# mLSTM scan of a two-layer token mixer: state terms and decayed scores one step ahead, the output-gate projection behind the scan without a barrier, another order of weight loads

## The chip, the cores and the metric

The kernel runs on one core of one Trainium2 chip. The core has five engines, each with its own instruction queue: TensorE (PE), VectorE (DVE), ScalarE (ACT), GpSimd (POOL) and SyncE (SP), which issues most of the DMA transfers. The metric is the device time of one execution in microseconds (us). The kernel before takes 2833.85 us, the median of three executions (2833.59 to 2839.1).

## The reference

A trunk of two layers works on 512 latent tokens and 256 context tokens of width 1024, in float32. Each layer has a token mixer and a mixture of 16 experts. The mixer projects its normalised input with one wide matrix (`w_in`) into the inputs of three branches: a bidirectional chunkwise mLSTM, a pooling mixer, and a neighbourhood attention. The change lies in the mLSTM and in the loads around it. One step of its scan is, for one direction and one chunk of 128 tokens:

```
b = cumsum(f); dmat = where(tril, b_t - b_s + i_s, -inf)
g = b + m;     mt = maximum(g, dmat.max(-1))
sc  = (q @ k.T) * exp(dmat - mt)                    # scores times decay: "S x D"
num = exp(g - mt) * (C @ q) + sc @ v                # C @ q: the state term, "qC"
den = exp(g - mt) * (n @ q) + sc.sum(-1)
h   = num / maximum(abs(den), exp(-mt))
C   = decay * C + sum_s ws_s * v_s k_s^T            # n likewise
out = sigmoid(o) * head_rms(h_forward + h_backward) # o: the output-gate projection
```

There are four heads, two directions and six chunks (two of context, then four latent; the backward direction goes through both sets in reverse). Layer 0 needs the output of every chunk; layer 1 needs only those of the four latent chunks, its context chunks serving for the state alone. The expert part gathers 64 latent rows per expert (in layer 0 also 32 context rows), runs a SwiGLU with three 1024 x 1024 matrices and adds the weighted rows to a buffer in DRAM.

## The kernel before, in words

The code is five queues written out by hand, one per engine, tied by semaphores. A layer is cut into phases. At the end of each, every engine drains its queue, adds one to the semaphore `phase` and waits until all four compute engines have (`phase_end`, L330 to L332). In a profile such a wait stands as L331 of the engine that came last.

A projection with a 1024 x 512 piece of `w_in` is done in two halves of 512 rows. A half is loaded by SP into a slot (1 MB), split into a rounded high part by ACT (`split`, L896) and a low part by POOL (L1612), and multiplied three times over (high x high, high x low, low x high, L409 and L414). There are three ring slots for weights. They hold, one after another, the halves of `w_in` (called qk, v, o, kn, qn, vn, pu after the branch they feed; o is the output gate, kn, qn and vn the attention's keys, queries and values, pu the pooling input) and twelve 2 MB pieces of the modulation weights (`ada`, L423). A load is issued by SP when the last user of its slot has signalled (`released`), and SP's queue is in order: a load whose slot is not free holds everything behind it.

The scan (phase 4) runs over n = 0 to 11: step n//2 of direction n%2. For an n with an output, the engines do this:

- PE: with eight of the n, one ada piece of 64 matmuls in pairs of partitions (L423); the state term qC into banks 2 and 3 (L577); the state's update kv from POOL's weighted values into bank 6 (L587); then the scores times values (`m_num`, L594) into banks 2 and 3 again, after ACT has taken qC out of them and DVE has written S x D; then the scores of the next output (L559).
- ACT: the scaled copy `qcs` of qC (four instructions, L997), the four exponentials of the next output's decay matrix (L984), and the broadcast load of a row of numbers for a later one (`u_load`, L946).
- DVE: S x D (L1344), the update of the state C (L1352, two), the sum nd of qcs and num (L1357), the denominator (L1360 to L1362), and the quotient into `hsum` (one instruction for the first direction to reach a chunk, L1365, four for the second, L1368).
- POOL: the masked rows for the decay (`masked`, L1633), the weighted values (L1643), and at the scan's end the low parts of the two halves of w_o.

After `phase_end(4)` the o projection runs over token tiles (6 in layer 0, 4 in layer 1), its first half of rows for all tiles and then its second. In the second half each tile is followed by `head_cols` of the tile before (L606), four transposes that need `hfin` from DVE (L1384), which needs the norm of `hsum` (L1373 to L1380) and ACT's sigmoid (L1017). Phases 5 and 6 end it and the projections kn, qn and vn. In the vn projection's second half ACT copies each finished tile out (L1058, L1060), the first four through POOL's DMA to `v_dram` (L1660) by way of two staging buffers; ACT's split of the second half of pu stands in its queue behind the wait for the second tile, and POOL's low part of it behind the fourth DMA.

In the expert loop six slots take the six 2 MB units of an expert. SP waits until the unit that used the slot is done, and then also until the load before the last one has landed, before it issues the next:

```
s2, back = (s - 2) % 6, 1 if s < 2 else 0
sp.wait_ge(w_ready(s2), 16 * e + 16 * (moe_base[l][s2] + 1 - back))
```

Of the kernel before, what the change touches and what calls it, by code (L numbers as in the profile page):

```python
# [4 lines left out]
F32 = mybir.dt.float32  # L5
# [69 lines left out]
def build(nc, A, out):  # L75
    ctx = ExitStack()
    with ctx:
# [121 lines left out]
        qcs = cut(zone, 28976, "p (h n) -> p h n", 516, h=MH)  # L199
# [82 lines left out]

        moe_base = []
        for l in range(DEPTH):
            n = [0]

            def nxt(key, src):
                add((l,) + key, src, n[0] % 3, None)
                n[0] += 1
            for j in range(4):  # L290
                nxt(("ada", l, j), kn512(ada[l], 512 * j))
            for name, c in (("qk", C_QK), ("v", C_V), ("o", C_O), ("kn", C_KN), ("qn", C_QN), ("vn", C_VN),
                            ("pu", C_PU)):
                for half in range(2):
                    nxt((name, half), w_in[l][512 * half:512 * half + 512, c:c + 512].rearrange("(k p) n -> p k n", p=P))
                if name == "v":
                    for j in range(4, 12):
                        nxt(("ada", l, j), kn512(ada[l], 512 * j))
            assert n[0] % 3 == 2
# [33 lines left out]
        NPH = 12  # L333
# [55 lines left out]
        def _(pe):  # L389
# [48 lines left out]
            for l in range(DEPTH):  # L438
# [114 lines left out]
                def pair_scores(u):  # L553
# [7 lines left out]
                    i.then_inc(sem("m_s"), 1)  # L561
                pair_scores(0)
                for n in range(12):
                    st, r = n // 2, n % 2
                    c = (FW, BWD)[r][st]
                    for j in range(4 + 2 * n // 3, 4 + 2 * (n + 1) // 3):
                        ada_unit(l, j, 1 if j < 8 else 0)
                    outp = c < nt(l)
                    if outp:
                        u = outs.index((r, c))  # L570
                        if st:
                            pe.wait_ge(sem("m_C"), l * PER["m_C"] + n - 1)
                        if u:
                            pe.wait_ge(sem("m_nd"), l * PER["m_nd"] + u)
                        for h in range(MH):
                            q0 = 64 * (h % 2)
                            i = mm(bank(2 + h % 2)[:, (h // 2) * 129:(h // 2) * 129 + 129],  # L577
                                   qT[q0:q0 + 64, h // 2, c * P:(c + 1) * P], Cst[q0:q0 + 64, r, h // 2, :],
                                   start=True, stop=True)
                        i.then_inc(sem("m_qc"), 1)  # L580
# [1318 lines left out]
```

## Time and profile before

| what | value |
|---|---|
| median of three executions | 2833.85 us |
| the profiled execution, its own time | 2833.22 us |
| its span, first to last instruction | 2831.1 us |
| mean granted TensorE clock, share of full speed | 0.937 |
| layer 0: scan's first kv to the o projection's first matmul | 152.77 to 230.72 us |
| layer 1: the same | 1682.42 to 1744.35 us |

All times of the trace are microseconds from the start of the span. 2.1 us of the profiled execution lie outside its span. In the rows further down, the chain of waits is the work that ended last, followed backwards and printed in order of time: start, duration, engine and line, with a count of merged instructions. "PEclk" is the TensorE clock that was granted: 1.00 is 2.4 GHz, 0.50 is 1.2 GHz.

### The profile page before, as it was taken

What the parts mean: (1) busy time and instruction counts of PE and PEld (TensorE: products, weight loads), DVE (VectorE), ACT (ScalarE), POOL (GpSimd) and SP (SyncE); (2) the same over time, 40 slices, a digit from 0 to 9 for tenths busy, and PEclk for the clock granted to TensorE, in tenths of its full rate; (3) what the DMA queues carried; (4) which work ended last, traced back from release to release, by engine and by line L of the source; (5) the groups of instructions that cost most, each with busy time, mean ns of one, the idle gap of its engine ahead of it and who ended that gap; (6) DMA issues with size and microseconds to landing.
All of it is one profiled execution on the core that took longest, in us unless ns stands there. A gap on an engine that the chain in (4) does not pass through costs nothing.

```text
span 2831.1 us, 38214 instructions
## 1 busy us (share of the span) xinstructions
PE 2411.7 (85%) x15894; PEld 1558.4 (55%) x15894; DVE 659.9 (23%) x1326; ACT 610.7 (22%) x1018; POOL 577.7 (20%) x320
## 2 busy tenths in 40 slices
PE   3987989899999499999997597988899868877775
PEld 2766867788884244444443476776688432322222
DVE  3255045311001511111111426046210130000002
ACT  3233233212111211111111424232321211000101
POOL 1133231224420001111111223331454000001000
PEclk7999999999999699999999799999999979999997
DMA  6261330111230589999999244431222469999997
GB/s 221 86 228 59 119 97 27 53 53 60 67 129 27 204 310 381 386 391 389 388 389 366 89 166 173 133 97 54 70 90 97 131 263 401 407 405 404 405 407 296
DMA packets 180453, 603.11 MB, mean 213 GB/s; under 512 B 14328, under 2 KB 55680, under 8 KB 167872
## 3 DMA queue, kind: packets, MB, share of 16 engines
q1 hardware_dynamic: 164704, 566.16, 53.2%
q0 software_dynamic: 12608, 30.19, 4.2%
q10 hardware_dynamic: 3040, 5.31, 0.6%
q8 instruction: 77, 1.26, 0.2%
q14 instruction: 24, 0.20, 0.0%
HBM read 579.51 MB, written 28.39 MB: 215 GB/s over the span
## 4 chain that ended last, share of the span: by engine, by line
PE 42%; DMA 37%; issue 8%; DVE 7%; ACT 3%; POOL 1%; SPq 1%; POOLq 1%; ACTq 0%; DVEq 0%
PE ps L414 15%; DMA ring_lo<-in_w_gate 12%; DMA zone<-in_w_down 10%; PE ps L409 9%; DMA zone<-in_w_up 6%; DMA ring_lo<-in_w_up 6%; PE ps L749 6%; PE ps L767 5%; PE ps L423 1%; PE ps L825 1%; DMA ring_lo<-in_ada_w 1%; DVE small L1417 1%; POOLq L331 1%; POOL zone L1676 1%; PE ps L594 1%
## 5 line engine op out<-in xcount | busy, mean ns | idle before, releaser
L825 PE MATMUL ps<-ring_lo,zone 128*32 128x256 f32 (+1 forms) x3072 | 460.1, 509 | 75.7 <-DMA ring_lo<-in_w_gate 43.2
L414 PE MATMUL ps<-hi_r,ring_r 128*128 128x512 f32 (+1 forms) x1792 | 477.3, 355 | 17.4 <-POOLq L331 14.8
L825 PEld LDWEIGHTS ps<-ring_lo,zone 128*32 128x32 f32 (+1 forms) x3072 | 167.1, 127 | 365.3 <-issue 337.8
L414 PEld LDWEIGHTS ps<-hi_r,ring_r 128*128 128x128 f32 x1792 | 318.8, 191 | 66.6 <-POOLq L331 16.5
L1612 POOL TENSOR_TENSOR ring_r<-ring_lo,ring_r 128x2048 fp32r<-128x2048 f32 x52 | 239.5, 4610 | 478.1 <-ACT ring_r L896 477.8
L414 PE MATMUL ps<-lo_r,ring_r 128*128 128x512 f32 (+1 forms) x896 | 316.7, 353 | 0.0
L835 PE MATMUL ps<-zone 128*64 128x512 f32 (+1 forms) x2048 | 289.6, 493 | 0.9
L409 PE MATMUL ps<-ring_r,hi_r 128*128 128x512 f32 x736 | 234.1, 400 | 21.7 <-DVEq L331 21.7
L835 PEld LDWEIGHTS ps<-zone 128*64 128x64 f32 (+1 forms) x2048 | 111.3, 124 | 162.3 <-issue 141.5
L1716 POOL DMA_INDIRECT zone<-xn_dram,zone x36 | 40.9, 1137 | 753.0 <-DVE zone L1587 667.3
L414 PEld LDWEIGHTS ps<-lo_r,ring_r 128*128 128x128 f32 x896 | 170.7, 191 | 23.7
L409 PEld LDWEIGHTS ps<-ring_r,hi_r 128*128 128x128 f32 x736 | 138.0, 191 | 50.9 <-DVEq L331 22.1
L825 PE MATMUL ps<-zone 128*32 128x256 f32 (+1 forms) x1024 | 146.8, 487 | 16.2 <-DMA zone<-in_w_up 16.2
L409 PE MATMUL ps<-ring_r,lo_r 128*128 128x512 f32 x368 | 145.2, 395 | 0.0
L1570 DVE COPY zone<-zone 128x2 f32 (+1 forms) x32 | 5.1, 161 | 593.0 <-POOLq L1737 593.0
L1486 DVE TENSOR_TENSOR zone<-zone,ps 128x768 f32<-128x768 f32 (+1 forms) x48 | 39.4, 821 | 426.4 <-ACT zone L1118 426.4
L767 PE MATMUL ps<-ring_lo,zone 128*128 128x512 f32 x320 | 137.7, 592 | 0.0
L1733 POOL DMA_INDIRECT moe_dram<-zone x48 | 74.9, 1559 | 273.1 <-issue 273.1
L749 PE MATMUL ps<-br_lo,ring_r 128*128 128x512 f32 (+1 forms) x480 | 125.7, 354 | 0.0
L896 ACT ACTIVATE ring_r<-ring_lo 128x2048 fp32r<-128x2048 f32 x48 | 91.7, 1915 | 133.5 <-DMA ring_lo<-in_w_in 112.8
L825 PEld LDWEIGHTS ps<-zone 128*32 128x32 f32 (+1 forms) x1024 | 56.6, 123 | 100.6 <-issue 89.4
L749 PE MATMUL ps<-br_up,ring_r 128*128 128x512 f32 (+1 forms) x384 | 103.1, 355 | 3.2 <-DVE br_lo L1478 3.2
(260 smaller groups left out, 2549.0 us busy)
## 6 DMA issues: line engine op xcount, KB each, us to landing
ring_lo<-in_w_gate SPq DMA_DIRECT2D x64, 2048.0 KB
zone<-in_w_down SPq DMA_DIRECT2D x64, 2048.0 KB, 10.1
ring_lo<-in_w_up SPq DMA_DIRECT2D x32, 2048.0 KB
zone<-in_w_up SPq DMA_DIRECT2D x32, 2048.0 KB, 11.7
ring_lo<-in_w_in SPq DMA_DIRECT2D x52, 1024.0 KB
ring_lo<-in_ada_w SPq DMA_DIRECT2D x24, 2048.0 KB
ring_lo<-in_w_branch SPq DMA_DIRECT2D x24, 512.0 KB, 6.1
zone<-v_dram SPq DMA_DIRECT2D x128, 64.0 KB, 1.9
```

Source lines behind the costliest of these rows:

```text
L331: eng.drain().then_inc(sem("phase"), 1)
L409: i = mm(dst, a[:, k, t * P:(t + 1) * P], b[:, kk, :], start=start and n == 0, stop=stop and n == 2)
L414: i = mm(dst[:, t0:t0 + tw], b[:, kk, f * P:(f + 1) * P], a[:, k, t0:t0 + tw], start=start and n == 0, stop=stop and n == 2)
L749: i = mm(pb[:, t0:t0 + tw], w[:, k, (f % 2) * P:(f % 2 + 1) * P], b[:, k, t0:t0 + tw], start=(k == 0 and x == 0), stop=(k == KB - 1 and x ...
L767: i = mm(PS[2 + t % 2][:, j * 512:(j + 1) * 512], acc[:, k, t * P:(t + 1) * P], w[:, k, :], start=(k == 0), stop=(k == KD - 1))
L825: i = mm(bank(((2, 4), (3, 5))[s // 2][gi])[j * M:(j + 1) * M, 0:W], xeT[:, k, c0:c0 + M], w[:, k % 4, j * W:(j + 1) * W], start=(k == 0), ...
L835: i = mm(bank((3, 5)[gi])[j * M:(j + 1) * M, 0:W], hidL[:, k % 4, k // 4, :] if gi == 0 else hidC[:, k % 2, k // 2, :], w[:, k % 4, j * W: ...
L896: A_(unit_hi(slot, ring_r), unit_lo(slot), ACT.Copy).then_inc(sem("w_hi"), 1)
L1486: V.tensor_tensor(dst[:, 0:TW(l)], sg[f % 2][:, 0:TW(l)], PS[(f % 2) * 2][:, 0:TW(l)], ALU.mult).then_inc(sem("mg_free"), 1)
L1612: G.tensor_tensor(unit_lo(slot, ring_r), unit_lo(slot), unit_hi(slot, ring_r).bitcast(F32), ALU.subtract)\
L1716: G.indirect_dma_start(xe[0:ns, :], None, xn_dram[l][0:TW(l), :], bass.IndirectOffsetOnAxis(ap=icur[0:ns, 0:1], axis=0)).then_inc(sem("xe_ ...
L1733: G.indirect_dma_start(moe_dram[l][0:TW(l), :].rearrange("t (j n) -> (t j) n", n=W), bass.IndirectOffsetOnAxis(ap=iprev[:, g:g + 1], axis= ...
```

## The change

The scan is reordered. PE issues the state term of n + 1 right behind the num of n, and the scores of the next output before this num; num gets banks 0 and 1 of its own. `qcs` has two buffers. DVE writes S x D of the next output ahead of the sum nd of this one. ACT has two decay matrices done before the barrier ahead of the scan, POOL three masked rows. The ada pieces stand at the end of eight steps, all in bank 7. The barrier between scan and o projection is gone (11 phases for 12); the o projection waits for single semaphores and uses banks 6, 7, 0, 1, 2, 3. POOL's low parts of w_o are made in four pieces of 512 columns each, the first one's inside the scan; ACT's `split(6)`, which works on kn's first half, now follows `split(5)` with no barrier between.

The loads have a table `ORDER` in place of a running count modulo three. o's first half is now loaded ahead of three of the ada pieces. By this table some halves get other slots: kn's first half takes the slot of o's first half, which is released when PE has finished the first half of the o projection (before: that of the last ada piece), and pu's second half takes slot 0, the one of vn's second half (before: the slot of vn's first half).

SP's second wait in the expert loop, on the load before the last one, is removed.

```diff
-        qcs = cut(zone, 28976, "p (h n) -> p h n", 516, h=MH)
+        qcs = [cut(zone, at_, "p (h n) -> p h n", 516, h=MH) for at_ in (28976, 27952)]
...
+        ORDER = ((("ada", 0), 0), (("ada", 1), 1), (("ada", 2), 2), (("ada", 3), 0), (("qk", 0), 1), (("qk", 1), 2), (("v", 0), 0),
...
+                 (("qn", 1), 1), (("vn", 0), 2), (("vn", 1), 0), (("pu", 0), 1), (("pu", 1), 0))
+        ADA_STEP = {0: 4, 1: 5, 2: 6, 4: 7, 5: 8, 7: 9, 8: 10, 10: 11}
+        O_BANKS = (6, 7, 0, 1, 2, 3)
...
+                def state_terms(n):
+                    st, r = n // 2, n % 2
+                    c = (FW, BWD)[r][st]
+                    u = outs.index((r, c))
+                    if st:
+                        pe.wait_ge(sem("m_C"), l * PER["m_C"] + n - 1)
+                    if u:
+                        pe.wait_ge(sem("m_qcs"), l * PER["m_qcs"] + u)
...
+                    if n in steps_out:
+                        u = outs.index((r, c))
                         if u + 1 < len(outs):
                             pair_scores(u + 1)
-                phase_end(pe, ph + 4)
+                        else:
+                            pe.wait_ge(sem("m_sd"), l * PER["m_sd"] + u + 1)
+                        if u:
+                            pe.wait_ge(sem("m_nd"), l * PER["m_nd"] + u)
+                        for h in range(MH):
+                            i = mm(bank(h % 2)[:, (h // 2) * 129:(h // 2) * 129 + 129], sdT[u % 2][:, h * P:(h + 1) * P],
+                                   v_ext[:, c, h, :], start=True, stop=True)
+                        i.then_inc(sem("m_num"), 1)
+                    if n + 1 in steps_out:
+                        state_terms(n + 1)
+                    if n in ADA_STEP:
+                        if ADA_STEP[n] == 8:
+                            pe.wait_ge(sem("ada_rows"), 3 * l + 2)
+                        ada_unit(l, ADA_STEP[n], 7)
...
+                    if n == 8:
+                        split(l, 4)
+                ada_rows(l, 2, 7)
                 split(l, 5)
-                phase_end(act, ph + 4)
                 split(l, 6)
...
+                def decayed_scores(u):
+                    dve.wait_ge(sem("m_s"), l * PER["m_s"] + u + 1)
+                    dve.wait_ge(sem("m_D"), l * PER["m_D"] + u + 1)
+                    V.tensor_tensor(by_parity(sdT[u % 2]), two(PS[2], P), by_parity(U[u % 3]), ALU.mult)\
+                        .then_inc(sem("m_sd"), 1)
...
+                w = 2048 // parts
+                for x in range(parts):
+                    i = G.tensor_tensor(unit_lo(slot, ring_r)[:, x * w:x * w + w], unit_lo(slot)[:, x * w:x * w + w],
+                                        unit_hi(slot, ring_r)[:, x * w:x * w + w].bitcast(F32), ALU.subtract)
+                i.then_inc(sem("w_lo"), 1)
...
+                    if n == 8:
+                        split(l, 4, 4)
+                split(l, 5, 4)
                 split(l, 6)
                 split(l, 7)
-                phase_end(pool, ph + 5)
+                phase_end(pool, ph + 4)
...
-
-                        s2, back = (s - 2) % 6, 1 if s < 2 else 0
-                        sp.wait_ge(w_ready(s2), 16 * e + 16 * (moe_base[l][s2] + 1 - back))
-                        sp.sem_inc(sem("sp_turn"), 1)
                         expert_unit(e, s)
```

PE's queue inside the scan of layer 0, before: one step with an ada piece (L423), its state term (L577), kv (L587), num (L594) and the next scores (L559).

```order
L423 MATMUL ps<-ring_lo,small 32x128 [waits w_ready2]
L423 MATMUL ps<-ring_lo,small 32x128 x31
L577 MATMUL ps<-zone 128x129 [waits m_nd,m_C]
L577 MATMUL ps<-zone 128x129 x3
L587 MATMUL ps<-zone 64x129 [waits m_C,m_vw]
L587 MATMUL ps<-zone 64x129 x3
L594 MATMUL ps<-zone 128x129 [waits m_qcs,m_sd]
L594 MATMUL ps<-zone 128x129 x3
L559 MATMUL ps<-zone 128x128 [waits m_sd]
L559 MATMUL ps<-zone 128x128 x3
```

The same place now: kv (L592), the next scores (L561), num (L604), the next state term (L575), and before them the ada piece of the step ahead (L425).

```order
L425 MATMUL ps<-ring_lo,small 32x128 [waits w_ready0,ada_rows]
L425 MATMUL ps<-ring_lo,small 32x128 x31
L592 MATMUL ps<-zone 64x129 [waits m_C,m_vw]
L592 MATMUL ps<-zone 64x129 x3
L561 MATMUL ps<-zone 128x128 [waits m_sd]
L561 MATMUL ps<-zone 128x128 x3
L604 MATMUL ps<-zone 128x129 [waits m_nd]
L604 MATMUL ps<-zone 128x129 x3
L575 MATMUL ps<-zone 128x129 [waits m_qcs,m_C]
L575 MATMUL ps<-zone 128x129 x3
```

The scores moved ahead of num and the state term behind it. num waits for the sum nd of the output before, no more for `qcs`.

SP's queue in layer 0, before, from the five ada loads of the scan to the first attention value load. The halves from `w_in` are o, o, kn (three waiting for ada_done), kn (half), qn (oproj), qn (half), vn (np), then behind the tables vn (half), pu (np) and pu (half), and the first piece of the merge weights (128x8x256).

```order
L1752 DMA ring_lo<-in_ada_w 128x8x512 [waits ada_done] x5
L1752 DMA ring_lo<-in_w_in 128x4x512 [waits ada_done] x3
L1752 DMA ring_lo<-in_w_in 128x4x512 [waits half]
L1752 DMA ring_lo<-in_w_in 128x4x512 [waits oproj]
L1752 DMA ring_lo<-in_w_in 128x4x512 [waits half]
L1752 DMA ring_lo<-in_w_in 128x4x512 [waits np]
...
L1752 DMA ring_lo<-in_w_in 128x4x512 [waits half]
L1752 DMA ring_lo<-in_w_in 128x4x512 [waits np]
L1752 DMA ring_lo<-in_w_in 128x4x512 [waits half]
L1752 DMA ring_lo<-in_w_in 128x8x256 [waits np]
L1778 DMA zone<-v_dram 32x512 [waits v_out1,v_out0]
```

SP's queue now, the same stretch.

```order
L1785 DMA ring_lo<-in_ada_w 128x8x512 [waits ada_done] x2
L1785 DMA ring_lo<-in_w_in 128x4x512 [waits ada_done]
L1785 DMA ring_lo<-in_ada_w 128x8x512 [waits ada_done] x3
L1785 DMA ring_lo<-in_w_in 128x4x512 [waits ada_done]
L1785 DMA ring_lo<-in_w_in 128x4x512 [waits half]
L1785 DMA ring_lo<-in_w_in 128x4x512 [waits ada_done]
L1785 DMA ring_lo<-in_w_in 128x4x512 [waits oproj]
...
L1785 DMA ring_lo<-in_w_in 128x4x512 [waits half]
L1785 DMA ring_lo<-in_w_in 128x4x512 [waits np] x2
L1785 DMA ring_lo<-in_w_in 128x8x256 [waits half]
```

kn's first half, the load behind o's second, waits for `half` (the end of the first half of the o projection) where it waited for an ada piece, and pu's second half waits for `np` (the last vn tile) where it waited for `half` (the end of vn's first half).

ACT's queue now, in the vn projection of layer 0: the copies out of the tiles, with the split of pu's second half (L917) between the first and the second. It stood at the same place before.

```order
L1080 ACTIVATE zone<-ps 128x512 [waits np]
L917 ACTIVATE ring_r<-ring_lo 128x2048 [waits w_ready0,np]
L1080 ACTIVATE zone<-ps 128x512
L1080 ACTIVATE zone<-ps 128x512 [waits v_out0,np]
L1080 ACTIVATE zone<-ps 128x512 [waits v_out1,np]
L1082 ACTIVATE zone<-ps 128x512 [waits np] x2
```

What moved is only the slot: the split waits for `w_ready0`, so for a load into the slot of vn's second half.

## Rows read from the trace of the kernel before

**Rows 1.** Chain of waits, layer 0: start, duration (us), engine, line, count.
```profile
152.77 1.13 PE ps L587 x8
196.65 1.13 PE ps L594 x8
197.78 0.65 PE ps L559 x8
198.43 1.88 PE ps L423 x64
200.31 0.67 PE ps L577 x8
218.72 1.14 PE ps L594 x8
221.30 9.33 DVE zone L1368 x4
230.72 24.84 PE ps L409 x96
272.78 67.15 PE ps L414 x384
339.93 16.36 PE ps L409 x72
```

**Rows 2.** Chain of waits, layer 1.
```profile
1682.42 1.13 PE ps L587 x8
1732.35 1.14 PE ps L594 x8
1744.35 18.70 PE ps L409 x72
1775.74 57.22 PE ps L414 x288
```

**Rows 3.** Stretches: bounds, length, busy us of each engine, PEclk, DMA share, GB/s.
```profile
175.00:205.00 30.00, 25.83 (x433) 21.41 (x432) 19.99 (x45) 11.98 (x41) 11.60 (x10) 0.94 0.80 283
230.00:236.00 6.00, 5.28 (x12) 4.18 (x13) 5.72 (x8) 3.19 (x2) 3.25 (x1) 0.50 0.00 0
```

**Rows 4.** Instructions of DVE: start, duration, line, operands, count.
```profile
204.19 0.86 DVE L1360 SCALAR_TENSOR_TENSOR small<-zone 128x4 f32<-128x4 f32 x1
262.74 3.70 DVE L1384 TENSOR_TENSOR zone<-zone 128x512 f32<-128x512 f32 x1 [1.90 <-ACT zone L1017]
```

**Rows 5.** Issues of SP, three merged: the first at 339.96.
```profile
339.96 33.93 SPq L1752 DMA_DIRECT2D ring_lo<-in_w_in  x3
```

**Rows 6.** Instructions of ACT, with idle time before them and its releaser.
```profile
232.63 1.28 ACT L1019 ACT_TABLE_LOAD   x1
243.01 0.32 ACT L1019 ACTIVATE small<-small 128x24 f32<-128x24 f32 x1 [9.10 <-DVEq L1375]
345.09 1.92 ACT L896 ACTIVATE ring_r<-ring_lo 128x2048 fp32r<-128x2048 f32 x1 [4.25 <-DMA ring_lo<-in_w_in]
373.54 0.60 ACT L1060 ACTIVATE zone<-ps 128x512 f32<-128x512 f32 x1 [2.12 <-PE ps L409]
```

**Rows 7.** Instructions of POOL in layer 0.
```profile
365.36 0.58 POOL L1660 DMA_DIRECT2D v_dram<-zone  x1 [3.74 <-ACT zone L1058]
369.55 4.61 POOL L1612 TENSOR_TENSOR ring_r<-ring_lo,ring_r 128x2048 fp32r<-128x2048 f32 x1
```

**Rows 8.** DMA issues of the page: KB each, median us from issue to landing.
```profile
v_dram<-zone POOLq DMA_DIRECT2D x8, 256.0 KB, 2.3
```

**Rows 9.** Stretches of the expert part, columns as in rows 3.
```profile
952.00:962.00 10.00, 6.62 (x38) 6.12 (x36) 8.22 (x18) 2.05 (x2) 0.00 (x0) 0.75 1.03 421
1317.00:1386.00 69.00, 67.33 (x608) 28.90 (x606) 7.85 (x22) 7.83 (x12) 8.10 (x6) 1.00 1.03 388
1338.00:1352.00 14.00, 13.13 (x116) 6.01 (x114) 2.87 (x9) 0.60 (x1) 0.22 (x1) 1.00 1.03 414
2559.00:2571.00 12.00, 9.55 (x37) 3.79 (x37) 0.97 (x3) 1.44 (x2) 0.00 (x0) 0.86 1.00 426
```

More of the change, by code:

```diff
@@ L561, in pair_scores @@
                     i.then_inc(sem("m_s"), 1)
+                def state_terms(n):
[7 more added lines that the diff above has]
+                    for h in range(MH):
+                        q0 = 64 * (h % 2)
+                        i = mm(bank(2 + h % 2)[:, (h // 2) * 129:(h // 2) * 129 + 129],
+                               qT[q0:q0 + 64, h // 2, c * P:(c + 1) * P], Cst[q0:q0 + 64, r, h // 2, :],
+                               start=True, stop=True)
+                    i.then_inc(sem("m_qc"), 1)
+                steps_out = [n for n in range(12) if (FW, BWD)[n % 2][n // 2] < nt(l)]
                 pair_scores(0)
+                if 0 in steps_out:
+                    state_terms(0)
                 for n in range(12):
@@ L987, in _ @@
                 decays(0)
+                decays(1)
+                phase_end(act, ph + 3)
                 for n in range(12):
@@ L991, in _ @@
                         u = outs.index((r, c))
-                        act.wait_ge(sem("m_qc"), l * PER["m_qc"] + u + 1)
-                        if u:
-                            act.wait_ge(sem("m_nd"), l * PER["m_nd"] + u)
-                        for h in range(MH):
-                            x0 = 129 * (h // 2)
-                            i = A_(qcs[:, h, :], bank(2 + h % 2)[:, x0:x0 + 129], ACT.Copy,
-                                   scale=xp0[:, r, 4 * (n // 2) + h:4 * (n // 2) + h + 1])
-                        i.then_inc(sem("m_qcs"), 1)
-                        if u + 1 < len(outs):
-                            decays(u + 1)
                         if u + 3 < len(outs):
@@ L1004, in _ @@
                             u_load(u + 3)
-                    if n == 6:
-                        ada_rows(l, 1, 1)
-                ada_rows(l, 2, 0)
-                split(l, 4)
+                        act.wait_ge(sem("m_qc"), l * PER["m_qc"] + u + 1)
+                        if u >= 2:
+                            act.wait_ge(sem("m_nd"), l * PER["m_nd"] + u - 1)
+                        for h in range(MH):
+                            x0 = 129 * (h // 2)
+                            i = A_(qcs[u % 2][:, h, :], bank(2 + h % 2)[:, x0:x0 + 129], ACT.Copy,
+                                   scale=xp0[:, r, 4 * (n // 2) + h:4 * (n // 2) + h + 1])
+                        i.then_inc(sem("m_qcs"), 1)
+                        if u + 2 < len(outs):
+                            decays(u + 2)
+                    if n == 5:
+                        ada_rows(l, 1, 7)
+                    if n == 8:
+                        split(l, 4)
+                ada_rows(l, 2, 7)
                 split(l, 5)
-                phase_end(act, ph + 4)
                 split(l, 6)
@@ L1602, in _, with split @@
             G = nc.gpsimd
-            def split(l, h):
+            def split(l, h, parts=1):
                 slot = units[(l,) + SPLITS[h]][1]
```

181 lines of the change are left out of this document (81 added, 100 removed).

## The prediction

> **What bounds the kernel now.** I read the chain of waits first, in order of time, and looked for stretches of the mixer in which PE doesn't follow PE. The scan of layer 0 is a relay: a step with an ada piece runs num, scores, ada piece, state term (1.13, 0.65, 1.88, 0.67 us) on PE, then waits for ACT's copy before the next num [rows 1]. From the first kv (152.77) to the end of the last num (219.86) it takes 67.1 us for twelve steps, 5.6 each; in layer 1, where four steps have no output, 51.1 us (1682.42 to 1733.49) [rows 1, 2]. The table of stretches shows that no engine is full there: of 30 us PE works 25.8 and DVE 20.0 [rows 3]. Behind each scan stands a hole of 10.9 us (219.86 to 230.72, 1733.49 to 1744.35): four small DVE instructions of the last step take 9.33 us beside POOL's low parts of w_o, and everybody waits at the barrier [rows 1, 2]. The o projection then starts at the lower of TensorE's two clock levels, 1.2 GHz (granted 0.50 in the first 6 us) [rows 3]. Its first 96 matmuls take 24.84 us; at 16.36/72 = 0.227 us each they would take 21.8 [rows 1].
>
> Next I followed the queues behind this place, ACT's and SP's, because the change alters which slot a half comes into. In the vn projection nothing waits for a load now: PE finishes its last tile at 373.54, POOL its low part of pu at 374.16, and the barrier falls 0.6 us behind PE [rows 6, 7].
>
> Last the expert part, most of the second and fourth quarter of the span. There the DMA engines are full (share 1.03) and in layer 0 PE too, 67.3 of 69 us [rows 9].
>
> **The change part by part.** All in the time of the profiled execution: 2831.1 us of span and 2.1 outside.
>
> *Scan.* A step with an ada piece becomes a PE queue without a wait: kv, scores, num, state term, ada piece. kv has no row of its own at full clock; as four matmuls of 129 columns like the state term I take 0.67. Sum 0.67 + 0.65 + 1.13 + 0.67 + 1.88 = 5.00 us. A step without one would take PE 3.1, but DVE worked 20.0 us in 30/5.6 = 5.4 steps, 3.7 us per step, and will be the longer one; with some waiting, 4.0. Layer 0: eight ada steps less one kv, 39.3; three of 4.0; last num 1.1: 52.5. The first step runs at the lower clock (its kv takes 1.13 now [rows 1]): about double, + 3.8. POOL's four pieces lie in steps 9 and 10; + 2. So 58.3, a gain of 8.8. Layer 1: three steps of kv and ada piece (7.7), one of kv and state term (1.3), four of 5.0, two of 4.0, 4.3 and 1.1, 42.4; cold 2.2, pieces 2: 46.6, a gain of 4.5. Together 13. The start itself I take as even: two masked rows go ahead of the barrier on POOL and as many exponentials on ACT. Bounds: nothing gained, if rows that are loaded for the decay now come late, to 27, if the steps are PE's alone and warm. 13 is between, nearest to the durations of rows 1.
>
> *Barrier.* With no phase end the o projection follows the last num. Its low part is made around step 9, and its first banks are free. Gain 2 x 10.9 = 21.7. PE stays warm: 24.84 - 21.8 = 3.0, and 18.70 - 72 x 0.227 = 2.3 in layer 1 [rows 1, 2]. Together 27. DVE's tail (its four quotients and the squares of hsum) now lies beside the first half of the o projection, 6 x 12 x 0.227 = 16.4 us in layer 0 and 10.9 in layer 1.
>
> *What is late next: kn's first half.* Its load waits for the end H of the o projection's first half, and ACT's split of it stands in ACT's queue ahead of the square root and of every sigmoid that the o projection's second half needs. A load of this kind issued at 339.96 was used at 345.09: 5.1 us [rows 5, 6]. Split 1.9, so H + 7.1. Then POOL makes the low part, 4.6, in one piece, and DVE's two instructions for `hfin` (scale and product, both with two inputs in SBUF) wait for it: H + 11.7, and 0.6 + 0.7 more (an instruction on 512 columns takes 0.6 on ACT [rows 6]; I take about that for DVE): H + 13.0. PE stands at `head_cols(0)` after two tiles, H + 5.5. It waits 7.5 us, and then I let it run at the lower clock as after the hole of before, 3 us. The later stall of before (3.70 us for a product beside POOL [rows 4]) I leave as it was. Cost 2 x 10.5 = 21. Bounds: 5 us per layer if DVE isn't held and PE stays warm, 13 if more waits.
>
> The rows behind this: a DVE instruction on four columns that takes 0.86 us [rows 4], and the 9.33 us of four on 128 columns [rows 1], each with two inputs in SBUF and each beside a POOL instruction. The Trainium skill ("SBUF — State Buffer", section "SBUF: two separate sides") says that VectorE with two SBUF inputs and GpSimd share a port pair as an exclusive lock for a whole instruction. The trace agrees. It speaks for the four pieces and against the uncut low part of kn that now starts just before `hfin`. By it hfin(0) comes at H + 13.0; without it, after table loads of 1.28 and a root of 0.32 [rows 6], at about H + 11, and the stall is 5.5 in place of 7.5, 4 us less over both layers.
>
> *pu's second half.* Its slot is now that of vn's second half, so SP can't load it before PE's last vn tile, T. But ACT's split of it stands behind the first of six copies. From T: load 5.1, split 1.9, copy of tile 1 0.5, to POOL's issue 0.3, transfer to `v_dram` 2.3 [rows 8] (the fourth copy needs this staging buffer), copy 0.7, 0.3, POOL's issue 0.6, and POOL's low part of pu, 4.6, which stands behind the DMAs [rows 7]. T + 16.3 in place of T + 0.6: 15.7 us per layer, 31 together. Nothing hides it: the barrier waits for ACT and POOL, and the attention starts behind it. Bounds: 28 (DMA latencies half hidden) to 35. The first load of the merge weights also waits longer, for the end of pu's projection, but the pooling on DVE is ahead of its use; cost nothing, or 3 us without that cover.
>
> *Expert loads.* SP's extra wait goes, so up to five loads are under way in place of two. With five and fewer under way at 952 to 962 the engines moved 421 GB/s at a share of 1.03; with two and no indirect transfer 414 in layer 0 and 426 in layer 1, shares 1.03 and 1.00 [rows 9]. The engines are full either way, and the bytes are the same: nothing. Bounds: layer 0 can gain what PE is idle, 1.7 of 69 us, 12 us over 15 experts; on the other side, the indirect transfers hold the mean down to 388 from 414, 6%, and if they were held up by a quarter as much again it would be 15 us.
>
> Sum: - 13 - 27 + 21 + 31 = + 12. The profiled execution would go from 2833.2 to 2845.3, and the median lies 0.6 above it: **2846 us**.
>
> **Rivals.**
> - *Deeper load queue pays.* For it: 421 over 414. Against it: layer 1 already has 426 with two under way, and the share is full. It would give layer 0 back 12 us: 2834. The Trainium skill ("DMA: Bandwidth & Descriptors", section "Where 436 GB/s comes from") has 436 GB/s as the ceiling of the 16 engines. By that layer 0 has 5% over its 414, more than PE's idle share lets it use, so PE's 12 us stay the limit.
> - *pu's load is not waited for.* If ACT's split is served in time, because vn's last tiles don't end what the slot's release waits for, the 31 us go and the change does what its words say: 2815, faster. Against it: the wait `w_ready0` in ACT's queue and `np` in SP's, both in the order of instructions. What decides is whether the load is issued before or after PE's last vn tile.
> - *Expert part slower.* Five loads ahead of gathers and read-add transfers: POOL's rows come late, 0.5 us per expert, 15 over 30: 2861. It decides once an expert's rows land after PE's last down matmul of the one before. Against it: nothing waits for them now.
> - *The scan doesn't speed up.* DVE held by POOL at each step, and the rows for the decays late: the 13 us shrink to 3: 2856.
> - *Both small stalls fall short.* The scan gains 20 and the stall at kn costs 14: 2832 to 2838.
>
> **How the numbers follow.** Forecast 0.54; deeper queue 0.13; no wait for pu's load 0.05; experts slower 0.09; scan no faster 0.11; small stalls short 0.08. About 0.2% (5.7 us) is what a measurement of this kernel can tell from no change. Faster than 2828.2: the second rival, 0.05, and a part of the first, of the last and of a sum of them, 0.10: 0.15. Within: the rest of the first and the last, and the lower edge of the forecast, 0.17. Slower 0.68. The range for 8 in 10 is 2829 to 2861; the forecast's own, from the bounds of stalls and scan, is 2838 to 2858.
>
> **What would show it.** In the profile after: no DVE instruction of 9 us and no hole before the o projection; num to num 5 us in the scan; PE idle about 7.5 us before `head_cols(0)` in both layers, released by DVE; ACT idle in front of its split of pu until 5 us after PE's last vn tile, and PE idle 16 us behind this tile; two experts of layer 0 in 69 us. I am wrong if PE follows on within 2 us after vn, or if the period of the experts moves by over 0.3 us.

## The result and the profile after

| | before | after |
|---|---|---|
| median of 13 executions each | 2834.84 us | 2840.72 us |
| ratio after to before, 95% interval | | 1.0019 [1.0011, 1.0028] |
| profiled execution, its span | 2831.1 us | 2835.4 us |
| mean granted clock | 0.937 | 0.935 |
| layer 0: scan's first kv to the o projection's first matmul | 78.0 us | 52.0 us |
| layer 1: the same | 61.9 us | 45.7 us |

The changed kernel is 0.19% slower, 5.4 us by the ratio, where 0.43% was forecast (2846); the time lies inside the range, and at the 0.2% that a measurement can tell. The stretch that the change is about became 42 us shorter, so some 46 us came in elsewhere.

The chain of waits of the changed kernel in layer 0, from the first kv to kn's first matmul (L592 is kv, L604 num, L411 the o projection, L619 the head transposes; it answers to [rows 1]):

```profile
153.32 1.06 PE ps L592 x8
...
163.09 6.63 DMA zone<-u_dram
...
171.81 6.28 DMA zone<-u_dram
...
181.34 1.95 PE ps L425 x64
...
204.21 1.13 PE ps L604 x8
205.34 16.36 PE ps L411 x72
...
221.72 5.14 DMA ring_lo<-in_w_in
...
226.88 1.91 ACT ring_r L917
...
228.81 1.28 ACT L1041
...
230.79 3.14 DVE zone L1406
...
233.95 0.70 DVE zone L1410
...
234.70 1.12 PE ps L619 x4
235.81 4.41 PE ps L411 x12
```

The hole of [rows 1] is gone: num ends at 205.34 and the o projection starts in the same moment, its 72 matmuls at 0.227 us each. Its first half ends at 221.70 (H), PE has two more tiles (to 227.2) and then waits; the first head transposes start at 234.70: H + 13.0, the number of the forecast. In layer 1 H is 1734.72 and they start at 1747.78, H + 13.1. Between lies the load of kn's first half, ACT's split of it, the square root and DVE's scale (L1406), which takes 3.14 us beside POOL's low part. The stretches of that wait and behind it (columns as in [rows 3]) have PE empty for 7.5 us, the size forecast, and then 6 us at a mean clock of 0.62:

```profile
227.20:234.70 7.50, 0.00 (x1) 0.01 (x1) 4.18 (x4) 5.56 (x6) 4.50 (x1) 0.85 0.21 80
234.70:240.70 6.00, 6.00 (x21) 5.02 (x22) 1.83 (x3) 1.04 (x2) 0.00 (x0) 0.62 0.00 0
```

Kn itself starts at 254.23, against 272.78 in [rows 1]. The scan of layer 1, whose last num ends at 1723.77 (it answers to [rows 2]), has a wait for an ada load in it:

```profile
1700.50 13.15 DMA ring_lo<-in_ada_w
...
1723.77 10.95 PE ps L411 x48
```

The same chain at the end of vn in layer 0 (it answers to [rows 6, 7]):

```profile
338.61 16.38 PE ps L411 x72
...
355.01 5.30 DMA ring_lo<-in_w_in
...
363.09 2.35 DMA v_dram<-zone
...
366.42 0.54 POOL v_dram L1693
366.96 4.94 POOLq L333
```

PE is done at 354.99 (T). Then everything is as the queue of ACT has it: load, split, copies, transfer, and POOL's low part, until 371.90, T + 16.9. In layer 1 it is T + 17.0. In the kernel before, PE paused here for 1.1 us in either layer (373.50 to 374.62 in layer 0; the 0.6 us of the prediction goes by the end of POOL's instruction, and the barrier opens 0.5 us behind that).

In the expert part of layer 0, the stretch of [rows 9] (columns as there):

```profile
1317.00:1386.00 69.00, 68.90 (x616) 29.46 (x614) 7.68 (x20) 7.83 (x12) 8.10 (x6) 1.00 1.03 391
```

PE is idle 0.1 us of 69 instead of 1.7, and the loads move 391 GB/s instead of 388.

From the start of one stage to the start of the next, the difference of the two profiled executions comes out like this (us, after less before; the o projection runs from its first matmul to kn's first, and "behind vn" is PE's pause between its last vn matmul and its next one):

| | layer 0 | layer 1 |
|---|---|---|
| scan | 52.0 - 67.1 = - 15.1 | 45.7 - 51.1 = - 5.4 |
| hole behind it | - 10.9 | - 10.9 |
| o projection | 48.9 - 42.1 = + 6.8 | 38.1 - 31.4 = + 6.7 |
| behind vn | 16.9 - 1.1 = + 15.8 | 17.0 - 1.1 = + 15.9 |
| experts, first to last matmul of gate and up | 528.0 - 532.1 = - 4.1 | 489.3 - 488.5 = + 0.8 |
| all other stretches | about + 5 over both | |

The named stages sum to - 0.4, and the spans differ by + 4.3, so all of the difference stands in the last row. That row is many small differences of 0.3 to 1.7 us between stages whose code is the same (the largest are the attention of layer 0, + 1.7, and of layer 1, + 1.0, and the way from layer 0's experts to layer 1's scan, + 1.0); it has no single cause that I could find.

### The profile page after: what moved, and what is told of

Its sections match the earlier page's. It is cut to its first block, busy times and chain, and to the rows that moved or that the text cites. A ratio compares the mean times of both kernels' runs of the same rounds, so it can differ in the third digit from the quotient of the medians.

```text
span 2835.4 us, 37864 instructions
## 1 busy us (share of the span) xinstructions
PE 2407.3 (85%) x15894; PEld 1555.2 (55%) x15894; DVE 654.6 (23%) x1326; ACT 611.2 (22%) x1018; POOL 581.1 (20%) x332
## 4 chain that ended last, share of the span: by engine, by line
PE 59%; DMA 21%; issue 8%; DVE 6%; ACT 3%; POOL 1%; SPq 1%; POOLq 1%; ACTq 0%; DVEq 0%
PE ps L416 15%; PE ps L846 14%; DMA ring_lo<-in_w_up 13%; PE ps L411 9%; PE ps L770 6%; PE ps L856 5%; PE ps L788 5%; DMA zone<-in_w_up 4%; DMA ring_lo<-in_ada_w 2%; PE ps L425 1%; POOLq L333 1%; DVE small L1443 1%; POOL zone L1709 1%; DMA ring_lo<-in_w_in 1%; PE ps L710 1%
## 5 line engine op out<-in xcount | busy, mean ns | idle before, releaser
L1640 POOL TENSOR_TENSOR ring_r<-ring_lo,ring_r 128x2048 fp32r<-128x2048 f32 (+1 forms) x64 | 241.6, 3784 | 467.2 <-ACT ring_r L917 466.9
L411 PE MATMUL ps<-ring_r,hi_r 128*128 128x512 f32 x736 | 232.6, 397 | 0.0
L1749 POOL DMA_INDIRECT zone<-xn_dram,zone x36 | 40.9, 1136 | 754.2 <-DVE zone L1613 667.6
L411 PEld LDWEIGHTS ps<-ring_r,hi_r 128*128 128x128 f32 x736 | 137.3, 190 | 28.5 <-issue 0.8
L411 PE MATMUL ps<-ring_r,lo_r 128*128 128x512 f32 x368 | 144.6, 393 | 0.0
L917 ACT ACTIVATE ring_r<-ring_lo 128x2048 fp32r<-128x2048 f32 x48 | 91.8, 1912 | 190.0 <-DMA ring_lo<-in_w_in 189.6
## 6 DMA issues: line engine op xcount, KB each, us to landing
ring_lo<-in_w_up SPq DMA_DIRECT2D x32, 2048.0 KB, 21.6
zone<-in_w_up SPq DMA_DIRECT2D x32, 2048.0 KB, 26.4
```

The source lines that it names most:

```text
L411: i = mm(dst, a[:, k, t * P:(t + 1) * P], b[:, kk, :], start=start and n == 0, stop=stop and n == 2)
L917: A_(unit_hi(slot, ring_r), unit_lo(slot), ACT.Copy).then_inc(sem("w_hi"), 1)
L1640: i = G.tensor_tensor(unit_lo(slot, ring_r)[:, x * w:x * w + w], unit_lo(slot)[:, x * w:x * w + w], unit_hi(slot, ring_r)[:, x * w:x * w + ...
L1749: G.indirect_dma_start(xe[0:ns, :], None, xn_dram[l][0:TW(l), :], bass.IndirectOffsetOnAxis(ap=icur[0:ns, 0:1], axis=0)).then_inc(sem("xe_ ...
```

## The experiments

A ratio is always to the kernel before on the same chip, and 1.0019 is the changed kernel's. 0.001 is 2.8 us.

**Expert loads alone.** The kernel before, with this taken out of SP's loop:

```
-    s2, back = (s - 2) % 6, 1 if s < 2 else 0
-    sp.wait_ge(w_ready(s2), 16 * e + 16 * (moe_base[l][s2] + 1 - back))
-    sp.sem_inc(sem("sp_turn"), 1)
```

> The kernel before with SP's second wait in the expert loop taken out and nothing else, so that five expert loads can be under way instead of two. My theory: the traces of before and after show layer 0's period fall from 34.4 to 33.4 us in most experts and layer 1's stay at 32.3, so about 3 us faster than before, all of it in layer 0's experts, nothing in layer 1 (2830 to 2833). Rival 1 (the forecast's own term): the engines are full either way, no difference to before within 1 us. Rival 2 (the gain in the changed kernel's experts comes from something else, such as an earlier start of the stage): no difference either, and the period of layer 0 stays at 34.4 us. Rival 3 (deeper queue pays in full): 12 us faster, 2823.

Measured: 2831.2, ratio 0.9983 [0.9972, 0.9994], 3 to 5 us faster than before. The chain of layer 0's experts in this kernel shows one expert from L835 to L835, 33.41 us, all of it PE:

```profile
1046.56 10.68 PE ps L835 x96
1057.24 21.22 PE ps L825 x192
1079.97 5.34 PE ps L835 x23
```

The chain of before, in a later part, passes only loads, one after the other, 34.4 us for each expert:

```profile
1317.56 11.90 DMA ring_lo<-in_w_gate
1329.60 11.96 DMA zone<-in_w_up
1341.73 10.08 DMA zone<-in_w_down
1352.02 11.80 DMA ring_lo<-in_w_gate
```

But the kernel before doesn't run at 34.4 us all along. From the start of one expert's gate matmuls to the next one's, it too takes PE's own 33.4 us for its second to ninth expert, and 34.1 to 34.5 for the six periods behind them; from 1000 to 1270 us PE is busy 269.6 of 270. Without the wait the 33.4 us last for eleven experts, here and in the changed kernel. Behind them the changed kernel's chain goes back to a load (26.6 us from issue to landing) and a period of 34.2. So in both kernels experts are served from a store of finished loads until it is used up, and then the engines' rate counts. The longer queue makes the store last three experts longer.

The throttle thus cost layer 0 about 4 us and layer 1 nothing that can be told (the changed kernel is 0.8 us longer there), and the rival that the queue pays the full 12 is wrong too. My forecast's zero was read from a share of 1.03, which hid those 1.7 us of idle PE that its own bound had named; and the bound of 12 took these 69 us for a sample of all 15 periods, where PE was idle in six.

**pu's split moved behind what needs ACT and POOL.**

```
 (ACT, vn copies)
-    if t == 1:
-        split(l, 13)
 (ACT, attention, step n)
+    if n == 3:
+        split(l, 13)
 (POOL: split(l, 13) from ahead of the barrier behind vn to behind the last bias)
```

> The changed kernel with the split of pu's second half moved to where it is no longer waited for at the end of the vn projection: ACT's part behind the fourth step of the attention, POOL's behind its last bias of the attention. Slots and loads stay as they are. My theory: the 16.9 and 17.0 us between PE's last vn tile and the barrier shrink to about 6 (copies of the last tiles and their transfers to DRAM still stand in front of it: 0.5 + 2.3 + 0.7 + 0.3 us and the POOL issue) or less, ACT pays up to 1.9 us in the attention: 20 to 31 us faster than the changed kernel, 2810 to 2821. Rival (the wait only moves: the attention's first loads or the pool step are late next): under 10 us. The stall in front of the first head transposes, 7.6 us per layer, stays.

Measured: 2820.76, ratio 0.9962 [0.9949, 0.9976], 16 us less than the changed kernel. The wait is gone: PE's last tile is finished at 353.4 and the barrier falls at 354.0. But 32 us went there, and the kernel is only 16 us faster. Of the rest some 13 are seen in the attention, which from this barrier to POOL's next instruction behind it (L1713) took 116.5 us; in the changed kernel it took 110.5, and in layer 1 95.5 against 88.0. The rows of the eighth kernel below, which has POOL's part at the same place, show where.

**Another table of slots.**

```
-    (("ada", 9), 2), (("ada", 10), 0), (("ada", 11), 2), (("o", 1), 0), (("kn", 0), 1), (("kn", 1), 2), (("qn", 0), 0),
-    (("qn", 1), 1), (("vn", 0), 2), (("vn", 1), 0), (("pu", 0), 1), (("pu", 1), 0))
+    (("ada", 9), 2), (("ada", 10), 0), (("o", 1), 2), (("ada", 11), 0), (("kn", 0), 0), (("kn", 1), 1), (("qn", 0), 2),
+    (("qn", 1), 0), (("vn", 0), 1), (("vn", 1), 2), (("pu", 0), 0), (("pu", 1), 1))
```

> The changed kernel with another table of slots: o's second half takes the slot of ada piece 9, so that kn's first half has the slot of the last ada piece and not of o's first half, and pu's second half has the slot of vn's first. Both are then loaded at least half a projection before ACT's split asks for them. My theory: the hole before the first head transposes (7.6 us and 2 us at the lower clock per layer) and the 16 us behind vn both go: 20 + 32 = up to 50 us less than the changed kernel, but DVE's product stays beside POOL's low parts somewhere, and a late low part of qn or vn may cost some: 2790 to 2800. Rival 1 (kn's stall comes from DVE's tail beside POOL, not from the load): only the 32 us of pu go: 2808, and PE still idle 7 us in front of the first head transposes. Rival 2 (only slots move the waits to qn or vn): over 2815.

Measured: 2800.76, ratio 0.9878 [0.9863, 0.9893], 40 us less than the changed kernel and 34 less than before. Both late loads go: in layer 0 the o projection takes 40.2 us instead of 48.9, and the barrier falls 1 us behind PE's last vn tile. The forecast's two minus terms were therefore real, and its two plus terms are the price of slots, not of the scheme. It falls short of the 50 in two places. The o projection yields 13 us of the 20 (layer 1: 34.0 us instead of 38.1): it still has DVE's 3.7 us product, and in layer 0 DVE's four last quotients take 7.3 us beside the pieces of w_o's second half and kn's uncut low part right behind them (5.0 in the tenth kernel, where kn's is in pieces too). And the table makes a new wait: ada piece 11 is loaded into the slot that piece 10 has just left. The chain of its scan in layer 0:

```profile
182.68 11.67 DMA ring_lo<-in_ada_w
194.40 2.00 PE ps L425 x64
196.41 7.62 DMA ring_lo<-in_ada_w
204.07 2.94 PE ps L425 x64
```

The scan takes 55.7 us there instead of 52.0, and 47.4 instead of 45.7 in layer 1.

**kn's first low part in four pieces.** In the changed kernel:

```
-    split(l, 6)
+    split(l, 6, 4)
```

> The changed kernel with POOL's low part of kn's first half made in four pieces instead of one; the load stays as late as it is. DVE's two instructions for the first output tile now wait behind the one long POOL instruction (first tile ready 13.0 us after the end H of the o projection's first half in both layers). My theory, which the Trainium skill's page "SBUF — State Buffer" (section "SBUF: two separate sides") supports with a lock held for one whole instruction: DVE gets in between two pieces, the first tile is ready at H + 10 to 11, the stall in front of the head transposes shrinks from 7.6 to about 5, and the kernel is 4 to 5 us faster than the changed one (2836), if the low part's own longer duration doesn't eat it. Rival (the load sets the stall alone, DVE isn't held): no difference, first tile at H + 13.

Measured: 2837.69, ratio 1.0019 [1.0008, 1.0029], the changed kernel's. Both theories are half right. DVE's rows (start, duration, operands) first of the changed kernel and then of this one:

```profile
230.79 3.13 DVE L1406 TENSOR_TENSOR zone<-zone,small 128x512 f32<-128x512 f32 x1
233.95 0.69 DVE L1410 TENSOR_TENSOR zone<-zone 128x512 f32<-128x512 f32 x1
```

```profile
231.19 1.11 DVE L1406 TENSOR_TENSOR zone<-zone,small 128x512 f32<-128x512 f32 x1
232.84 1.14 DVE L1410 TENSOR_TENSOR zone<-zone 128x512 f32<-128x512 f32 x1 [0.54 <-ACT zone L1039]
...
244.02 3.69 DVE L1410 TENSOR_TENSOR zone<-zone 128x512 f32<-128x512 f32 x1 [1.92 <-ACT zone L1039]
```

Beside pieces the scale takes 1.11 us instead of 3.13, so the trace bears out the rule of the Trainium skill ("SBUF — State Buffer", section "SBUF: two separate sides") that the lock lasts one whole instruction. But then DVE waits 0.54 us for ACT's sigmoid, which stands behind a second table load of 1.28 us, and its product takes 1.14 us beside a piece: the first tile comes at H + 11.8 instead of H + 13.0. And the 3.7 us beside the low part of kn's second half is still there. The long instruction was worth 1 us here, and nothing in the total, because two other things were nearly as late.

**The barrier put back.** The changed kernel with

```
+    phase_end(pe, ph + 4)      (and on DVE, ACT and POOL; later phases + 1)
```

> The changed kernel with the phase end between the scan and the o projection put back on the four compute engines (PE behind the last ada piece, DVE behind the last quotients, ACT and POOL behind their split of o's second half); the order of the scan, the slots and the pieces stay. This measures the forecast's term of 27 us for the barrier by itself. My theory: DVE's tail of the last step ends 6.2 us behind the last num in the profile of the changed kernel (205.34 to 211.5), and PE restarts at the lower clock (2 to 3 us): 8 to 9 us per layer, 16 to 18 slower than the changed kernel, 2857. The forecast's term would want 27, 2868. Rival (the hole is only moved, because kn's late load and DVE's tail are paid behind the barrier anyway): under 8 us, 2848 or less.

Measured: 2858.41, ratio 1.0086 [1.006, 1.0113], 19 us above the changed kernel. Its chains in layer 0 and layer 1:

```profile
208.43 2.90 DVE zone L1397 x4
...
211.42 18.24 PE ps L411 x72
```

```profile
1736.68 5.13 DVE zone L1397 x4
...
1741.91 13.80 PE ps L411 x48
```

The hole is 6.3 and 6.8 us and the o projection's first half is 1.9 and 2.9 us longer, since it starts at the lower clock: 17.8. So the barrier by itself is worth 18. The rest of the forecast's 27 is DVE's shorter tail: the four DVE instructions had already gone from 9.33 us [rows 1] to 2.9 and 5.1. Two things did that, and no run parts them cleanly. Before, the tail stood beside both low parts of w_o (220.94 to 229.94 on POOL); now the first of them is made inside the scan. And the second is in pieces. In the sixth kernel, where the first is as early and the second is in one instruction, the four take 5.46 us in layer 0. By that some 4 us of the 6.4 come from the earlier first half, and 2.5 from the pieces.

**The pieces taken away.** The changed kernel with `split(l, 4, 4)` and `split(l, 5, 4)` turned to `split(l, 4)` and `split(l, 5)` on POOL.

> The changed kernel with the low parts of both halves of w_o made by POOL in one instruction each instead of four. My theory: DVE's two-input instructions of steps 9 and 10 and of the tail wait up to 4 us behind each; the first falls in the scan, where PE waits for DVE, 2 to 4 us per layer; the second in DVE's tail, which nothing waits for now: 4 to 8 us slower than the changed kernel, 2845 to 2849. Rival (the barrier's removal alone took the held instructions off the path, the pieces are worth nothing): the same time within 2 us.

Measured: 2845.71, ratio 1.0035 [1.0019, 1.0051], 4.5 us above the changed kernel, though the two intervals overlap. Its chain in layer 0:

```profile
194.49 6.39 DVE zone L1395 x4
...
202.89 1.81 PE ps L604 x8
```

Four quotients take 6.39 us beside POOL's first low part, PE waits for them before its eleventh num, and the scan 55.0 us instead of 52.0; in layer 1 it takes 49.3 instead of 45.7.

**A full rotation, and what can be added to it.** Ada pieces 9 to 11 come ahead of o's halves, and the split of o's first half one step later:

```
+    (("ada", 9), 1), (("ada", 10), 2), (("ada", 11), 0), (("o", 0), 1), (("o", 1), 2), (("kn", 0), 0), (("kn", 1), 1), (("qn", 0), 2),
+    (("qn", 1), 0), (("vn", 0), 1), (("vn", 1), 2), (("pu", 0), 0), (("pu", 1), 1))
```

> The changed kernel with another table: ada pieces 9 to 11 are loaded ahead of o's halves and all halves rotate through the slots (o's first half follows ada piece 9, its second ada piece 10, kn's first ada piece 11, pu's second vn's first); ACT's and POOL's split of o's first half stand one step later. In the table of the third experiment ada piece 11 had the slot of ada piece 10, and the chain of waits there showed PE waiting for two ada loads of 11.7 and 7.6 us (span 2802.8). My theory: these waits go, 3 to 4 us in layer 0 and 1 to 3 in layer 1, so 4 to 7 us less than with that table, 2794 to 2797, if the load of o's first half, now issued after step 7, is in before the last num. Rival (loads of this part share the DMA engines with the decay rows, and the sum of bytes sets the end of the scan): the same 2801, or slower, if o's first half comes late.

Measured: 2800.71, ratio 0.9876 [0.9852, 0.9899]: the same as the third kernel. In layer 0 the scan takes 51.3 us instead of 55.7. In layer 1 it takes 50.4 instead of 47.4: its chain passes 11.05 us of the load of o's first half, which ACT's split waits for ahead of the next copies `qcs`. That is the last clause of the rival, o's first half coming late.

The eighth kernel has `split(l, 6, 4)` and `split(l, 7, 4)`, and POOL's `split(l, 13)` behind its attention loop:

> As the kernel of the seventh experiment, and POOL makes the low part of pu's second half behind its attention loop instead of ahead of the barrier behind vn, and kn's low parts in four pieces each. My theory: the barrier behind vn falls about 1 us behind PE's last tile and not 6.7 us as in the third experiment (345.8 to 352.4), 5 us per layer; and DVE's product of the second output tile (3.7 us) takes 1 to 1.5 us: 2 us per layer. Together 12 to 14 us less than the seventh experiment: 2781 to 2785. Rival (POOL's later low part or the pieces hold DVE's masks and maxima in the attention or kn's own start): only 5 to 6 us less.

Measured: 2801.32, ratio 0.9882 [0.9861, 0.9904]. My reading of the third kernel's tail was wrong: I had taken an ACT copy at 345.8 for PE's last tile, which ends at 351. There was 1 us to win, not 5. And the low part inside the attention costs. DVE's rows beside it (first fence), and PE's next 16 matmuls of L710, with the same 16 later in the attention (second fence):

```profile
417.66 4.98 DVE L1453 TENSOR_SCALAR zone<-cst,small 128x128 f32<-128x128 f32 x2
422.56 0.68 DVE L1465 COPY zone<-ps 128x512 f32<-128x512 f32 x1
```

```profile
425.36 3.71 PE ps L710 x16
...
436.02 2.00 PE ps L710 x16
```

This pair takes 0.48 us where no POOL instruction stands beside it (426.75), and 0.72 beside one of POOL's short biases. PE stands idle meanwhile, from 418.77 to 423.38, and then runs at a granted clock of 0.50 until 429.07, the level of 1.2 GHz: its 32 matmuls of L727 and L710 take 5.69 us, and 3.08 in the tenth kernel, where nothing held DVE. The attention took 116.4 us, as in the second kernel, against 108.6 in the seventh. Some 4.3 us of that are the pair's, and 2.6 the lower clock's.

The tenth kernel takes that one move back and keeps kn's pieces:

> The kernel of the seventh experiment with kn's low parts in four pieces each, and POOL's low part of pu back at its place ahead of the barrier behind vn. In the eighth experiment the attention of layer 0 took 116.4 us between its barriers instead of 108.4, and vn's barrier fell only 1.6 us behind PE's last tile in the seventh. My theory: POOL's low part inside the attention cost the eighth what the pieces won: DVE's product of the second tile no longer takes 3.7 us, 2 to 3 us per layer, so 4 to 6 us less than the seventh, 2795 to 2797. Rival (the pieces win nothing, as in the fourth experiment, since something else comes last): 2801.

Measured: 2792.70, ratio 0.9852 [0.9832, 0.9872]: the fastest here, 42 us below before and 47 below the changed kernel. Its chain at the head transposes of layer 0 (L411 x12 is one output tile):

```profile
228.52 2.74 PE ps L411 x12
...
231.69 2.76 PE ps L411 x12
...
238.07 2.78 PE ps L411 x12
...
243.73 6.50 PE ps L416 x26
```

No stall of 3.7 us and no lower clock is left. The o projection takes 38.2 us in layer 0 and 29 in layer 1 (40.9 and 34 in the seventh kernel, 48.9 and 38.1 in the changed one). The pieces that were worth nothing with a late load are worth 7 to 8 us without it, by the traces and by the medians; the two timed intervals overlap.

**Decay rows loaded earlier.** Four buffers instead of three, first in the changed kernel, then in the tenth:

```
-    U = [... for i in range(3)]
+    U = [... for i in range(3)] + [cut(zone, 6656, None, 512)]
-    if u + 3 < len(outs): ... u_load(u + 3)
+    if u + 4 < len(outs): ... u_load(u + 4)
```

> The changed kernel with four buffers for the decay rows of the scan instead of three (the fourth in a part of the zone that is free there), so that a row is loaded one output earlier; nothing else changes. In the profile of the changed kernel the chain of waits of layer 0's scan passes two loads of decay rows (6.6 and 6.3 us) with POOL's mask and ACT's exponentials behind each, and PE stands until 181.3; in layer 1 it passes one ada load instead. My theory: these rows, requested too late, are what keeps the scan of layer 0 at 52.0 us instead of some 43 (eight ada steps of 4.9, three of 3.1 and the last num, less a kv): one of the two loads goes, so 4 to 8 us less in layer 0, 0 to 2 in layer 1: 2833 to 2837. Rival 1 (ada loads are behind them and come in at their own pace): less than 2 us. Rival 2 (the four first rows now share the engines with the ada loads and each takes longer): 2 us more.

> The kernel of the tenth experiment with four buffers for the decay rows. My theory: a further 4 to 8 us less in layer 0 (the chain of the seventh experiment passes two loads of rows, 6.1 and 6.4 us): 2788 to 2792. Rival (all halves and ada pieces come through the same engines, and the first half of o, loaded last, is late next): no more than 2 us less.

Measured: 2838.22, ratio 1.0015 [1.0002, 1.0028], and 2793.01, ratio 0.9858 [0.9833, 0.9883]: no difference to either. The loads of rows do leave the chain of layer 0, but they had cost PE little: in the changed kernel it was busy 15.57 of the 16.3 us up to 181.3. In the ninth kernel the chain reads like this (num, ada piece, num):

```profile
160.47 1.09 PE ps L604 x8
162.21 1.88 PE ps L425 x64
...
165.33 1.09 PE ps L604 x8
...
170.19 1.09 PE ps L604 x8
...
173.16 1.09 PE ps L604 x8
```

A step with an ada piece takes 4.86 us and one without 2.97, without a wait. The scan is 50.3 us instead of 52.0. The theory's 43 was also a wrong addition: its own terms make 49. What layer 1's scan waits for is seen in its chain, where the last stretch before the o projection passes

```profile
1684.29 12.73 DMA ring_lo<-in_ada_w
1699.16 12.90 DMA ring_lo<-in_ada_w
```

two ada loads of 2 MB, each as long as 2.6 steps.

## Why the prediction was right, and where its sizes were off

- *Scan, - 13.* It gained 20.5. Layer 1's 45.7 us are within 1 us of the 46.6, for another reason: PE waits in it for an ada load (1700.50 to 1713.65). The term was mis-sized by 7.5 us, 6.3 of them in layer 0. There I put 4.0 us for a step without an ada piece, since DVE's mean of 3.7 us per step seemed the limit. It takes 2.97, as the ninth kernel shows: 3 us over three steps. DVE worked 27.2 us in 175 to 205 here, and held PE once, 1.2 us before the last num (204.21). A step with an ada piece takes 4.86 and not 5.00, 1 us over eight. And the start at the lower clock cost some 2 us by its rows and not 3.8. The last rival had this gain of 20, with a smaller stall at kn that did not come.
- *Barrier and warm start, - 27.* The hole went (- 21.8) and the start is warm. As forecast; but the barrier by itself is worth 18 of it (the fifth kernel), and the other 9 are DVE's shorter tail, by the earlier low part of w_o's first half and by the pieces. In the scan the pieces are worth a further 4 to 5 (the sixth), if two overlapping intervals may be compared.
- *kn's first half, + 21.* The hfin time H + 13.0 and H + 13.1 is exact, the clock cost less: the next tile took 4.41 us instead of 2.73 and the one behind it 2.77, 2 us and not 3. The o projection is 6.8 and 6.7 us longer than before; with the 3.0 and 2.3 us of warm start that makes 9.8 and 9.0, 19 in all.
- *The lock's share of it, 4 us.* With pieces it was 1.2 us in either layer, 2.4 together. The first tile then comes at H + 11.8 and not at about H + 11: the sigmoid that the product needs stands behind the second table load, and DVE is still held for a piece.
- *pu's second half, + 31.* + 31.7. The order of ACT's queue decides it, and the table can undo it: the second, third and seventh kernel show it from both sides.
- *Expert loads, 0.* 4 us were gained in layer 0, inside the bounds. The step that failed was to take full DMA engines as a proof that nothing could be had while the same group of rows showed PE idle 1.7 us of 69. By the prediction's own sign this term was wrong: the period moved by more than 0.3 us, from 34.4 to 33.4, but for three experts only, since the others before them ran at 33.4 already.
- *Sum.* - 20.5 - 21.8 + 13.5 + 31.7 - 3.3 = - 0.4, and + 4.7 in stretches that the change doesn't touch, which I had at nothing. The forecast + 12 less the scan's 7.5, the experts' 3.3 and the kn stall's 2.2, with these 4.7 and the 0.7 that the vn tail has above 31, makes 4.4, and the spans differ by 4.3.
- *What was luck.* The mechanism holds: the two late loads eat what scan and barrier win, and with both gone the same change is 34 us faster than before. But the forecast's plus of 12 was more than twice the 5.4 measured, and by the named stages alone the two kernels would be even. That the kernel came out slower, and not the same, rests on 4.7 us whose cause is open.

## What to carry to other kernels

When a table of slots is changed, ask of every load what must be over before it may start, and which in-order queue asks for it next: two entries decided here whether the change cost 5 us or won 34. A wait is not gone when it is moved to a busy engine's queue (some 13 of 32 us came back in the attention); it is gone when its load is earlier. And a small fix can be worth nothing beside a later event and 7 us once that is gone, so it is to be tried again at the end.

## What the hardware showed that I had not expected

- A pair of DVE instructions with only one tensor operand, the other being a number per partition (TENSOR_SCALAR, 128x128, L1453), is held by a POOL instruction just as those with two full tensors: 4.98 us for two beside POOL's low part of 4.49, and 0.48 alone.
- With up to five loads of 2 MB under way each takes 21.6 to 26.4 us from issue to landing, where the page of before has 10.1 and 11.7 with two; the sum moved grows only from 388 to 391 GB/s.
- A pause of 7.5 us in front of the head transposes, and of 6.3 and 6.8 in front of the o projection (the fifth kernel), left PE at the lower clock for some 4 to 6 us by the granted clock of the stretches behind them (0.50 over the first 4.3 us behind the head transposes' start; 0.65 and 0.50 over the first 5 us of the two o projections), a loss of 1.9 to 2.9 us beside the pause. One of 4.6 us in the attention (the eighth kernel) did the same for 5.7 us. That granted clock is 1.2 GHz where a row shows 0.50, 2.4 where it shows 1.00.
